# A hybrid attention layer: projections laid out anew over the attention steps, rotary chunk and branch waits rearranged

## The reference

```python
h = rms_norm(x, g_pre_mix) * (1.0 + scale_m) + shift_m
qa, ka, va, qb, kb, vb, f_logit, gate_logit = split(h @ w_in)
qa, ka = rope(qa, positions), rope(ka, positions)
o_a = sliding_window_gqa_sinks(qa, ka, va, sinks)      # 8 heads, 2 kv heads, window 128
log_f = log_sigmoid(f_logit + b_f)
o_b = forgetting_attention(qb, kb, vb, log_f)          # 8 heads, causal, bias cum(log_f)
gates = sigmoid(gate_logit)                            # 2 x 1024 channels
merged = gates[0] * (o_a @ w_branch_a) + gates[1] * (o_b @ w_branch_b)
x = x + gate_m * rms_norm(merged @ w_out, g_post_mix)
# then the FFN: silu(h @ w_g) * (h @ w_u) @ w_down
```

## Time and profile before

| | us |
|---|---|
| median of 3 runs | 1571.97 |
| the runs | 1569.59 to 1573.26 |
| the profiled execution | 1568.9 |
| its span in the profile | 1567.2 |
| TensorE busy | 1494.8 |
| GpSimd, VectorE, ScalarE busy | 631.1, 575.0, 407.6 |

### The profile page before, as it was taken

One profiled execution on the slowest core, in us unless ns is written; L12 is line 12 of the kernel. 1 busy time (PEld: TensorE's weight loads), 2 busy tenths in 40 slices (PEclk: granted clock), 3 DMA queues, 4 the chain that ended last, 5 costly groups with the idle time before them and its releaser, 6 DMA issues.

```text
span 1567.2 us, 18736 instructions
## 1 busy us (share of the span) xinstructions
PE 1494.8 (95%) x7301; PEld 1221.6 (78%) x7301; DVE 575.0 (37%) x912; ACT 407.6 (26%) x834; POOL 631.1 (40%) x512
## 2 busy tenths in 40 slices
PE   4899998989989999999999999999999999999998
PEld 1898776677777888888787888888888887888886
DVE  3776876555544764767553000000000000003002
ACT  3711466555551001002343000000000002433331
POOL 0315734233363534344023332333323334975860
PEclk9999999999999999999999999999999999999999
DMA  9301101021213644333232111111111122434521
GB/s 351 108 14 29 64 25 47 35 68 35 101 55 99 164 135 135 108 108 107 85 117 64 57 40 54 42 52 54 40 54 44 50 67 83 145 108 124 172 95 54
DMA packets 145493, 132.67 MB, mean 85 GB/s; under 512 B 13104, under 2 KB 125832, under 8 KB 144912
## 3 DMA queue, kind: packets, MB, share of 16 engines
q1 hardware_dynamic: 139200, 126.96, 26.1%
q10 hardware_dynamic: 6224, 4.77, 0.9%
HBM read 119.10 MB, written 12.62 MB: 84 GB/s over the span
## 4 chain that ended last, share of the span: by engine, by line
PE 86%; DVE 6%; ACT 3%; POOL 2%; DMA 2%; issue 1%; SPq 0%; ACTq 0%; DVEq 0%; POOLq 0%
PE PS L1421 68%; PE PS L1545 9%; PE PS L1599 2%; DVE s_row L1174 2%; PE PS L1624 2%; PE PS L1651 1%; POOL s_row L674 1%; DMA wada<-in_w_ada_dram 1%; PE PS L1652 1%; PE PS L1432 1%; PE PS L1443 1%; ACT pt_hi L843 1%; DVE pt_lo L1193 1%; DMA w2raw<-in_w_ffn_out_dram 0%; PE PS L1603 0%
## 5 line engine op out<-in xcount | busy, mean ns | idle before, releaser
L1421 PE MATMUL PS<-act_hi,w_hi 128*128 128x512 f32 x928 | 361.9, 390 | 0.0
L1421 PE MATMUL PS<-act_hi,w_lo 128*128 128x512 f32 x928 | 361.1, 389 | 0.0
L1421 PE MATMUL PS<-act_lo,w_hi 128*128 128x512 f32 x928 | 361.1, 389 | 0.0
L634 POOL TENSOR_TENSOR w_lo<-wraw,w_hi 128x1024 fp32r<-128x1024 f32 x81 | 200.3, 2472 | 6.5
L1421 PEld LDWEIGHTS PS<-act_hi,w_lo 128*128 128x128 f32 x928 | 174.2, 188 | 36.3
L1421 PEld LDWEIGHTS PS<-act_lo,w_hi 128*128 128x128 f32 x928 | 174.2, 188 | 36.1
L1421 PEld LDWEIGHTS PS<-act_hi,w_hi 128*128 128x128 f32 x928 | 174.2, 188 | 35.7
L1397 DVE TENSOR_TENSOR act_ff<-PS,sl 128x512 f32 x40 | 27.7, 692 | 407.6 <-PE PS L1421 407.6
L632 POOL CAST w_hi<-wraw 128x1024 fp32r<-128x1024 f32 x81 | 85.9, 1060 | 183.2 <-PE PS L1421 113.0
L1421 PE MATMUL PS<-w_hi,ah_hi 128*128 128x512 f32 x352 | 137.1, 390 | 2.2 <-POOL w_lo L734 2.2
L970 ACT ACTIVATE sl<-PS 128x512 f32<-128x512 f32 x44 | 26.4, 600 | 429.2 <-PE PS L1421 429.2
(11 more groups left out here) (235 smaller groups left out, 2498.8 us busy)
## 6 DMA issues: line engine op xcount, KB each, us to landing
wraw<-in_w_ffn_in_dram SPq DMA_DIRECT2D x44, 512.0 KB
w2raw<-in_w_ffn_out_dram SPq DMA_DIRECT2D x44, 512.0 KB, 3.5
adaraw<-in_w_ada_dram SPq DMA_DIRECT2D x32, 512.0 KB, 3.9
wraw<-in_w_in_dram SPq DMA_DIRECT2D x25, 512.0 KB
wada<-in_w_ada_dram SPq DMA_DIRECT2D x6, 1024.0 KB, 15.1
xin<-in_x_dram SPq DMA_DIRECT2D x8, 512.0 KB, 7.2
cs<-ncum_dram SPq DMA_DIRECT2D x4, 1024.0 KB, 4.7
woraw<-in_w_out_dram SPq DMA_DIRECT2D x8, 512.0 KB, 4.5
```

The lines of the kernel that those rows point to most:

```text
L634: pool.tensor_tensor(w_hl[1][:, slot], wraw[:, slot], w_hl[0][:, slot].bitcast(F32), ALU.subtract)\
L1421: ins = nc.tensor.matmul(out_ap, lhs[a], rhs[b], start=first and i == 0, stop=last and i == 2)
```

## The change

1. **The table of a pair's projections.** Per step of a pair, matmuls of its four chunks before: 4, 5, 5, 5, 5 | 4, 4, 4, 4, 4, 4 | 4, 4, 4, 4, 4, 4, 0 | 4, 5, 5, 5, 5, none at k = 23; in the last pair 4 a step up to k = 17, none at 18, 4 or 5 from 19 to 23. After: 5, 6, 6, 6, 1 (first chunk), 9, 6, 5, 4 (second), 5, 5, 4, 4, 2, 4 (third), 0, 7, 3, 4, 3, 4, 3, 0, 0 (fourth), in all four pairs. The steps at which chunks are taken out are k = 5, 9, 15, 22 (last pair 6, 9, 15, 22); before 5, 11, 17, 23 (last pair 6, 12, 18, 24).
2. **Order in TensorE's stream.** `between` also holds at k = 5, and where it holds the projection matmuls too come after the transposes.
3. **The first branch's chunks.** Chunk 9 is taken at step 3, its five rotary products one a step from -1 to 3; chunk 10 goes from steps 3, 5, 7 to 5, 7, 9 and is taken at 10; chunk 13 from 23, 25, 27 to 26, 28, 30 and is taken at 31.
4. **Denominators** of rows 0 and 1 at steps -5 and -3 instead of -3 and -1.
5. **`branch(0)`**: each accumulator waits for what used its own bank.

```diff
     def den_step(r):
+        if r < 2:
+            return 2 * r - 5
         return s_step[r] + (3 if r < A_T else 2)
...
-    fills = {7: ([-7], -5), 8: ([-5], -3), 9: ([-3], -1), 10: ([3, 5, 7], 9), 11: ([11, 13, 15], 16),
-             12: ([17, 19, 21], 22), 13: ([23, 25, 27], 28)}
-    for pb in range(B_P - 1):
-        for nth, (start, steps, gap) in enumerate(((0, 5, 5), (5, 6, 11), (11, 6, 17), (18, 5, 23))):
-            fills[14 + 4 * pb + nth] = ([step0(pb) + start + i for i in range(steps)], step0(pb) + gap)
-    for nth, (start, steps, gap) in enumerate(((0, 6, 6), (6, 6, 12), (12, 6, 18), (19, 5, 24))):
-        fills[N_PROJ + nth] = ([step0(B_P - 1) + start + i for i in range(steps)], step0(B_P - 1) + gap)
+    fills = {7: ([-7], -5), 8: ([-5], -3), 9: ([-3], 3), 10: ([5, 7, 9], 10), 11: ([11, 13, 15], 16),
+             12: ([17, 19, 21], 22), 13: ([26, 28, 30], 31)}
+    LAST_ROPE = {-1: (0,), 0: (1,), 1: (2,), 2: (3,), 3: (4,)}
+    PAIR_FILL = ({0: 5, 1: 6, 2: 6, 3: 6, 4: 1}, {5: 9, 6: 6, 7: 5, 8: 4},
+                 {9: 5, 10: 5, 11: 4, 12: 4, 13: 2, 14: 4}, {16: 7, 17: 3, 18: 4, 19: 3, 20: 4, 21: 3})
+    PAIR_EVAC = ((5, 9, 15, 22), (6, 9, 15, 22))
...
+    for pb in range(B_P):
+        first = 14 + 4 * pb if pb < B_P - 1 else N_PROJ
+        for nth, counts in enumerate(PAIR_FILL):
+            gap = step0(pb) + PAIR_EVAC[pb == B_P - 1][nth]
+            made = 0
+            for k, count in counts.items():
+                mm_at[step0(pb) + k].append((first + nth, made, made + count))
+                made += count
+            assert made == 3 * KD
+            evac_at[gap].append(first + nth)
+            fills[first + nth] = (list(counts), gap)
...
-            def rope_products(j):
+            def rope_products(j, parts=range(5)):
...
+                if gp in LAST_ROPE:
+                    rope_products(N_ROPE - 1, LAST_ROPE[gp])
                 for j in evac_at[gp]:
-                    if j < N_ROPE:
+                    if j < N_ROPE - 1:
                         rope_products(j)
+                    elif j == N_ROPE - 1:
+                        continue
...
-                between = 0 <= gp < 2 * A_T and gp % 2 == 0
+                between = 0 <= gp < 2 * A_T and gp % 2 == 0 or gp >= 2 * A_T and (gp - 2 * A_T) % (3 * NTOK) == 5
                 for r in range(N_S):
                     if issue_step[r] == gp and not between:
                         scores(r)
-                for j, first, end in mm_at[gp]:
-                    project(j, first, end)
+                if not between:
+                    for j, first, end in mm_at[gp]:
+                        project(j, first, end)
                 if 0 <= gp + 1 < NG:
                     transpose_p(gp + 1)
-                for r in range(N_S):
-                    if issue_step[r] == gp and between:
-                        scores(r)
+                if between:
+                    for r in range(N_S):
+                        if issue_step[r] == gp:
+                            scores(r)
+                    for j, first, end in mm_at[gp]:
+                        project(j, first, end)
                 if gp >= 0:
                     times_v(gp)
...
                 if q == 0:
                     pe.wait_ge(proj_taken, N_PROJ)
                     pe.wait_ge(s_taken, N_S)
-                    pe.wait_ge(o_taken, len(o_step))
-                    pe.wait_ge(grp_lo, NG)
                 for j in range(4):
+                    if q == 0 and j < 2:
+                        pe.wait_ge(grp_lo, NG - 1 + j)
+                    elif q == 0 and j == 2:
+                        pe.wait_ge(o_taken, len(o_step))
```

More of the change, by code:

```diff
@@ L1114, in rope_products @@
                 before = [i for i in range(j) if rope_slot(i) == rope_slot(j)]
-                dve.wait_ge(proj_ready, j + 1)
-                if j == 0:
-                    dve.wait_ge(tables, 2)
-                if before:
-                    dve.wait_ge(rope_done, before[-1] + 1)
-                nc.vector.tensor_tensor(rope_a[:, :], PS[:, bank], cs[:, 0, cols], ALU.mult)
-                for quad in range(4):
-                    o, i = 32 * quad, 32 * (quad ^ 1)
+                if 0 in parts:
+                    dve.wait_ge(proj_ready, j + 1)
+                    if j == 0:
+                        dve.wait_ge(tables, 2)
+                    if before:
+                        dve.wait_ge(rope_done, before[-1] + 1)
+                    nc.vector.tensor_tensor(rope_a[:, :], PS[:, bank], cs[:, 0, cols], ALU.mult)
+                for part in parts:
+                    if part == 0:
+                        continue
+                    o, i = 32 * (part - 1), 32 * ((part - 1) ^ 1)
                     ins = nc.vector.tensor_tensor(rope_b[o:o + 32, :], PS[i:i + 32, bank], cs[i:i + 32, 1, cols], ALU.mult)
-                ins.then_inc(proj_taken, 1)
+                if 4 in parts:
+                    ins.then_inc(proj_taken, 1)
             dve.wait_ge(bc_in, 64)
```

## The result

| | before | after |
|---|---|---|
| median of the runs | 1573.28 us (1569.59 to 1573.68, 6 runs) | 1560.68 us (1558.92 to 1562.98, 6 runs) |
| profiled execution, its span | 1568.9, 1567.2 us | 1560.18, 1558.5 us |

The ratio is 0.9927 with a 95% interval of 0.9916 to 0.9939: the change saves 11.5 us (9.6 to 13.2). The forecast was 1559.7.

The account below looks back on a forecast made before the run. TensorE, busy 1494.8 of 1567.2 us, was taken as the bound, so only its holes could be won. Head -0.6, tail 4.0, pairs 4.1 and last pair 4.8 sum to 12.3 us saved: 1559.7 us, range 1554 to 1569.

Parts of the forecast that it names:

- Head: First branch, steps -5 to 12: 0.6 us slower, bounds 1.9 us faster and 2.5 slower.
- Tail: First branch, steps 22 to 32: 4.0 us gained, bounds 1.5 and 5.4.
- Pairs: Pairs 0, 1 and 2: 1.36 us gained in each, 4.1 for three; bounds for each 0 and 2.3.
- Last pair: Last pair, up to the first branch product: 4.8 us gained, including 1.8 from that product's wait for the last copy-out.
- The hole at 23: Step 23 of the first branch, which loses its chunk 13 matmuls: about 2.1 us of hole opens there.
- Everything after attention moves up unchanged: The dense TensorE work behind attention: it starts earlier and is otherwise unchanged.
- Attention ends near 474 us: Sign that the forecast is right: in the new trace, attention ends near 474 us.
- Light steps bound by the other engines: Rival: ScalarE and VectorE need 0.3 us more in some 20 three-matmul steps; gain only 6.3 us, 1565.7; chance 0.18.
- The clock at new holes: Rival: the granted clock falls at new holes, up to 3 us each, all nine 27 us, 1587; chance 0.06.
- nine named places: New holes: k = 5 in four pairs, three pair ends, steps 23 and 0 to 4 of the first branch.
- Waits passed on: Rival: head and pair ends lose what the middle wins; within 3 us of before, 1571; chance 0.09.
- The branch wait stays: Rival: something else holds the first branch product; 1.6 us less gain, 1561.3; chance 0.07.

Follow-up runs that it names:

- chunk 10 run: The changed kernel with the last rotary chunk's parts pressed into steps -1 to 1 and chunk 10 back on steps 3, 5, 7, taken at 9: 1560.71 us.
- old head run: The changed kernel with the first branch's early denominators, last rotary chunk and chunk 10 back at their old steps: 1559.51 us, ratio 0.9927.
- before again: The kernel before, unaltered, run once more for a second profiled execution: 1569.15 us, against 1568.9 in its first profile.
- branch wait only: The kernel before with one edit, first branch products waiting only for the accumulators they write: 1571.83 us against 1572.81, ratio 0.9991.
- first branch only: The kernel before with only the first branch's edits (denominators, rotary parts, chunks 10 and 13, projection behind transposes in even steps): 1569.56 us against 1572.81.

## Why the prediction was right

The forecast took 12.3 us off attention. From the first scores to the first branch product the two profiles have 333.92 and 322.92 us: 11.0 gained (11.4 against before's second profile), where the runs say 11.5 for the whole kernel. By the prediction's steps, counting each matmul moved across a border at 0.23 us, this is -0.8 + 3.3 + 3.9 + 4.6. Of the missing 1.3 us the tail has 0.7, and head, pairs and last pair have 0.2 each:

- **Head, forecast 0.6 slower: 0.8.** Product 0 lost its wait of 2.36, product 2 got one of 2.50, product 6 stayed (40.43 us after the first scores against 40.32), products 6 to 12 took 0.7 more. The chunk 10 run shows that this is chunk 10's place, and the old head run that nothing later pays for it. The loads that go out later show no cost: steps 12 to 22 take 27.19 us against 27.14.
- **Tail, forecast 4.0: 3.3** (3.06 and one matmul). Steps 24 to 32 gained 4.3, 0.5 more than I had: the fall at 260 us went as forecast, and product 29 waited 0.17 us where I had 1.0. But steps 22 to 24 took 7.00 us instead of 5.77. The hole at 23 was forecast at 2.1 us and is 1.6 (1.08, and 0.54 ahead of the transposes before it). That the clock would fall behind it (0.69 at 240 to 245) was priced only as a bound. That is the mis-sized term, worth 1.3 us by the two traces with the hole filled and the one with the hole and no fall. Against before's second profile the tail gained 1.3 us more, by that trace's fall at 250 us.
- **Pairs, forecast 1.36 each: 1.40, 1.27, 1.28.** By the products of k = 0, 8, 16 and the next k = 0, at 0.23 us a matmul, in the third pair: 24.16 us became 24.36 with seven more matmuls, 1.4 gained (forecast 0.46 + 0.91); 15.66 became 14.95 with one less, 0.5 gained (0.55); 15.66 became 14.89 with six less, 0.6 lost (-0.68 and 0.12). The wait at k = 5 is 1.26, forecast 1.2. The order at k = 5 is worth 0.4 us of each pair: without it the pair would have gained 0.9. From the end of row 3's scores to the next pair's first product it is 8.82 us, forecast 8.8; but of the new waits forecast at products 21 to 23 the trace shows only one, of 0.25 us at product 22, so the sum came out better than its parts.
- **Last pair, forecast 4.8: 4.6** (4.82 us, with one matmul less in it: the one that the tail has more). Up to its product of k = 8, 24.96 became 24.36 us with 11 more matmuls, 3.1 (forecast 3.2, 0.8 of it the clock's). That 0.8 belongs to the one profile and not to the change: three of the four traces with the old table of the pairs (before again, branch wait only, first branch only) have no fall at 455 us, and against before's second profile the last pair gained 4.07 us instead of 4.82. From there on 28.23 became 24.01 with 12 less, 1.5 (forecast 1.6); the branch wait alone gives 1.77 (forecast 1.8).
- **"Everything after attention moves up unchanged"** is true of the instructions and false of a single execution's time: 1079.4 to 1084.3 us over thirteen traces of the same code. The spans of the two profiles differ by only 8.7 us, because the changed kernel's lost 1.6 there and 0.7 ahead of the first scores, in code that is the same. "Attention ends near 474 us" did not follow from the prediction's own sum, which puts the first branch product at 487.79 - 12.3 = 475.5; it came at 477.52.
- **Rivals.** Light steps bound by the other engines: they are at the pair's end, priced at 0.68 and found at 0.6, not in 20 places. The clock at new holes: of the nine named places step 23 fell, in six traces of seven; none at k = 5 or a pair's end in any trace with the new table; steps 0 to 4 have a fall in every trace, before's too. They were priced at up to 3 us each; where two traces differ by one fall, it costs 0.75 us (last pair) to 1.3 us (250 us, step 23). The Trainium skill's warning that short, frequent gaps can make the clock swing ("TensorE: Matmul & The Clock Gate", A second HAM failure mode: psum-queue depth-cycling) agrees with the new hole at step 23 and not with those at k = 5 and the pairs' ends, where the granted clock stayed at 1.00. Waits passed on: only the head does it, from product 0 to product 2. The branch wait stays: excluded by the run with that edit alone.

That the forecast median is within 1 us of the measured one is partly luck. The gain was 0.8 too large against the runs' 11.5, and before's median, 1571.97 in the runs shown, came out at 1573.28 beside the changed kernel. These two would put the changed kernel 2.1 us above the forecast; its median came out only 1.0 above, well within the 9.6 to 13.2 us that the runs leave for the gain.

## What to carry to other kernels

Where all fill is the same work, count it per stretch between two waits: a matmul under a wait that another engine ends is free, and the same matmul moved to a step that TensorE ends is its full price. A new hole is not only its own length: the clock may fall behind it, at step 23 for another 1.3 us, so put a few matmuls into it before taking them all away. What a fall costs depends on what lies under it: in the chunk 10 run eight matmuls of step 3 took 1.3 us more under one. And read an edit's worth from segments of the trace that start at the changed place; a profile's total holds several microseconds of falls and load waits that belong to no edit. A gain that one profile promises from a clock fall is sure only if a second profile of the same kernel has that fall too.

## What the runs showed of the hardware

- The same instructions with the same idle gaps meet a fall of the granted clock in one execution and not in another. Around 840 us (start of the FFN) three of thirteen traces had none, ten lost 1.0 to 2.3 us. Before's first profile fell at 455 us, its second at 250. The holes of 1.03 to 1.48 us at k = 5, four in each of nine traces, never brought one.
- At the FFN's second product the wait for a split weight was 1.30 to 3.84 us. Behind it the clock fell in five traces (waits of 2.50 to 3.84) and not in eight (1.30 to 2.52, and one of 3.15), and the rest of the kernel then took 238.0 us instead of 236.4: the two lengths don't mix.
- A small VectorE operation that begins while GpSimd is in an operation ends with it. The same 128x4 statistic took 0.95 us at 180 us and 0.16 at 197. In the traces of before, of the changed kernel and of chunk 10 at old steps, up to 300 us, there are 26 such 128x4 operations (the statistic, its difference from the sink, the denominator's sum) that began with 0.16 us or more of a GpSimd operation still to run; all 26 ended 0.01 to 0.02 us after it, having taken 0.20 to 1.84 us. All others took at most 0.17 us. The row maximum ahead of the slower statistic, read from PSUM, took 1.23 us beside busy GpSimd and 1.22 at 196 us. No run varied GpSimd's work to test it.

```profile
180.42 1.04 POOL L644 CAST w_hi<-wraw 128x1024 fp32r<-128x1024 f32 x1
...
180.52 0.95 DVE L1172 SCALAR_TENSOR_TENSOR nm<-mx,nsink 128x4 f32<-128x4 f32 x1
...
197.44 0.16 DVE L1172 SCALAR_TENSOR_TENSOR nm<-mx,nsink 128x4 f32<-128x4 f32 x1
```
